# The last feed-forward's up projections of a two-block transformer kernel as seven block products, with the features between the projections split beside the second of them

## The reference

```python
x = x + jnp.concatenate([attn, pooled], axis=-1) @ w_out[l]
x = x + 0.5 * swiglu(rms_norm(x, ffn2_norm[l]), ffn2_w_gate[l], ffn2_w_up[l], ffn2_w_down[l])
# swiglu(x, g, u, d) = (silu(x @ g) * (x @ u)) @ d;  1024 -> 2816 twice, 2816 -> 1024
```

## Time and profile before

| | us |
|---|---|
| median of 3 runs (lowest, highest) | 2365.52 (2364.51, 2366.09) |
| span of the profiled execution | 2362.9 |
| TensorE busy in it | 2328.1 |
| VectorE, ScalarE, GpSimd busy | 1200.3, 878.0, 468.8 |
| TensorE's granted clock, mean share of full | 0.999 |

### The profile page before, as it was taken

One profiled execution on the slowest core, in us unless ns is written; L12 is line 12 of the kernel. 1 busy time (PEld: TensorE's weight loads), 2 busy tenths in 40 slices (PEclk: granted clock), 3 DMA queues, 4 the chain that ended last, 5 costly groups with the idle time before them and its releaser, 6 DMA issues.

```text
span 2362.9 us, 27596 instructions
## 1 busy us (share of the span) xinstructions
PE 2328.1 (99%) x11083; PEld 1893.2 (80%) x11083; DVE 1200.3 (51%) x1817; ACT 878.0 (37%) x1362; POOL 468.8 (20%) x475
## 2 busy tenths in 40 slices
PE   7999999999999999999999999999999999999999
PEld 5888877888787877777888888888887868888887
DVE  6555765555324456635545336444335984444423
ACT  4322345554223447733323234233225353323321
POOL 0111523445002048800000010000011870000000
PEclk9999999999999999999999999999999999999999
DMA  8664035656223210023233232333332212333322
GB/s 295 189 200 146 1 114 163 191 183 187 92 96 105 90 57 2 1 63 98 89 98 98 98 97 91 98 98 96 100 101 88 81 36 81 95 94 97 98 98 80
DMA packets 169333, 247.41 MB, mean 105 GB/s; under 512 B 14889, under 2 KB 110694, under 8 KB 169206
## 3 DMA queue, kind: packets, MB, share of 16 engines
q1 hardware_dynamic: 156276, 200.93, 26.5%
q0 software_dynamic: 12624, 44.54, 6.1%
q10 hardware_dynamic: 306, 0.19, 0.0%
HBM read 243.51 MB, written 2.10 MB: 104 GB/s over the span
## 4 chain that ended last, share of the span: by engine, by line
PE 87%; DVE 6%; POOL 3%; issue 2%; ACT 1%; DMA 1%; ACTq 0%; SPq 0%; POOLq 0%; DVEq 0%
PE ps L586 79%; DVE dsa_mask L2547 1%; POOL hg_k L2798 1%; PE ps L1050 1%; DVE w_lo L1957 1%; POOL nsa_p L2888 1%; PE ps L1066 1%; DVE small L2545 1%; DVE h_lo L2054 1%; PE ps L558 1%; PE ps L1040 0%; PE ps L1039 0%; PE ps L1281 0%; POOL nsa_b L2857 0%; PE ps L966 0%
## 5 line engine op out<-in xcount | busy, mean ns | idle before, releaser
L1957 DVE TENSOR_TENSOR w_lo<-w_raw,w_hi 128x1024 fp32r<-128x1024 f32 (+2 forms) x358 | 445.8, 1245 | 1004.7 <-ACT w_hi L1373 1004.4
L1373 ACT ACTIVATE w_hi<-w_raw 128x1024 fp32r<-128x1024 f32 (+2 forms) x364 | 380.7, 1046 | 1088.7 <-PE ps L586 1088.4
L586 PE MATMUL ps<-h_hi,w_hi 128*128 128x512 f32 (+1 forms) x1928 | 756.9, 393 | 4.9 <-DVE w_lo L1957 3.3
L586 PE MATMUL ps<-h_lo,w_hi 128*128 128x512 f32 (+1 forms) x1928 | 750.6, 389 | 0.0
L586 PE MATMUL ps<-h_hi,w_lo 128*128 128x512 f32 (+1 forms) x1928 | 750.4, 389 | 0.0
L586 PEld LDWEIGHTS ps<-h_hi,w_hi 128*128 128x128 f32 (+1 forms) x1928 | 361.3, 187 | 93.7 <-issue 7.6
L586 PEld LDWEIGHTS ps<-h_hi,w_lo 128*128 128x128 f32 (+1 forms) x1928 | 361.4, 187 | 76.4
L586 PEld LDWEIGHTS ps<-h_lo,w_hi 128*128 128x128 f32 (+1 forms) x1928 | 361.5, 187 | 75.9 <-issue 1.7
L586 PE MATMUL ps<-hid_hi,w_hi 128*128 128x512 f32 x616 | 240.9, 391 | 0.0
L586 PE MATMUL ps<-hid_lo,w_hi 128*128 128x512 f32 x616 | 239.7, 389 | 0.0
L586 PE MATMUL ps<-hid_hi,w_lo 128*128 128x512 f32 x616 | 239.7, 389 | 0.0
(11 more groups left out here) (397 smaller groups left out, 2570.0 us busy)
## 6 DMA issues: line engine op xcount, KB each, us to landing
w_raw<-in_ffn_w_up SPq DMA_DIRECT2D x264, 256.0 KB, 3.0
w_raw<-in_ffn_w_down SPq DMA_DIRECT2D x176, 256.0 KB, 2.8
m_raw<-in_ada_w POOLq DMA_DIRECT2D x80, 512.0 KB, 4.4
w_raw<-in_ffn_w_gate SPq DMA_DIRECT2D x88, 256.0 KB, 2.8
w_raw<-in_hg_w_in SPq DMA_DIRECT2D x64, 256.0 KB, 3.1
w_raw<-in_nsa_w_in SPq DMA_DIRECT2D x40, 256.0 KB, 2.9
w_raw<-in_w_in SPq DMA_DIRECT2D x32, 256.0 KB, 2.8
m_acc<-in_ada_w SPq DMA_DIRECT2D x9, 512.0 KB, 6.7
```

The source lines that it names most:

```text
L586: ins = K.nc.tensor.matmul(out, lhsT, rhs, start=start, stop=stop)
L1373: K.nc.scalar.activation(K.half(K.w_hi[u % SPL], width), K.half(K.w_raw[u % RAW], width), ACT.Copy) \
L1957: K.nc.vector.tensor_tensor(K.half(K.w_lo[u % SPL], width), K.half(K.w_raw[u % RAW], width), hi, ALU.subtract) \
```

## The change

It concerns `ffn_d` alone; elsewhere only names change. Gate and up weights by the two halves of the 1024 input features are a 2 x 2 matrix of blocks a11 (gate, first half), a12 (gate, second half), a21, a22 (up); the features by the early and the late 256 tokens are b11, b12, b21, b22. Instead of eight block products, a group makes seven (Strassen's scheme in Winograd's form), each 24 matmuls with 256 columns: the feature sums t1 to t4 are made once, the weight sums s1 to s4 for every group on GpSimd, from raw weights in float32, and the products' sums partly in PSUM, partly on VectorE.

- **Products** (`PRODUCTS`, `fast_order`): p1 = a11 b11, p5 = s1 t1, p6 = s2 t2, p7 = s3 t3, p4 = a22 t4, p3 = s4 b22, p2 = a12 b21. In groups 2 to 10 in the order p1, p6, p7, p5, p4, p3, p2; the first two groups begin with p1, p5 of group 0 and p1, p5 of group 1, which need the first half of the features alone. p4 is added in the bank of p7, p3 in that of p5, p2 in that of p1, each after that bank's first value has been read.
- **ScalarE**: split of product n + 3 into one of three pairs of buffers, then the copy of p1 out of PSUM (`u2`), and a group's Silu in one operation of 1024 elements.
- **VectorE**: the low part of product n + 3 ahead of what follows product n: the additions out of PSUM (u2, u3, up1, up0, gate1), the factors on the gate (gate0, gate2), the gating of 1024 elements.
- **GpSimd**: `third` (s3), `first` (s1), `second` (s2), `fourth` (s4) and `scaled` (the factors on the up half), 1024 elements each; before the first group also t1, t3 and t4 in two parts each.
- **SP**: four loads of 512 KB for a group into eight raw buffers, instead of eight of 256 KB into four.
- **The features between the projections** are kept in float32 (`hid`) and are split for each unit of the down projection, into a ring of two, by 1024 elements on ScalarE and on VectorE (`scalar_hid_high`, `vector_hid_low`), twice over, once for each half of the output. The first pair's low part is queued on VectorE after gate2 of group 10 and ahead of its gating.

The core of the diff; left out are the names of semaphores, the bookkeeping of loads and slots (`raw`, `hi`, `lo`, `raw_free`), and `hid_items`, which lists the down projection's matmuls as before over the ring.

```diff
+        self.hid = sb("hid", [P, KF, S], at=ar)
+        place = {"b11": ar + 45056, "t1": ar + 53248, "t2": ar + 61440, "t3": self.h_at, "t4": self.h_at + 8192,
+                 "b22": self.h_at + 16384, "b21": self.h_at + 24576}
+        self.feat = {n: sb(f"feat_{n}", [P, 4, 2, 256], F32R, at=at) for n, at in place.items()}
+        self.ring_hi = [sb(f"ring_hi{j}", [P, 2, S], F32R, at=self.h_at + 8192 * j) for j in range(2)]
+        self.ring_lo = [sb(f"ring_lo{j}", [P, 2, S], F32R, at=self.h_at + 8192 * j + 4096) for j in range(2)]
+        self.w_raw += [sb(f"w_raw{RAW + j}", [P, 1024], at=ar + 69632 + 4096 * j) for j in range(RAW)]
+        self.gate_buf = sb("gate_buf", [P, 2, S], at=ar + 86016)
+        self.u2 = [sb(f"u2_{j}", [P, 2, 256], at=ar + 90112 + 2048 * j) for j in range(2)]
+        self.s3, self.s2 = [sb(f"s3_{j}", [P, 1024], at=m + 16384 + 4096 * j) for j in range(2)], sb("s2", [P, 1024], at=m + 24576)
+        self.w_hi.append(sb("w_hi2", [P, 1024], F32R, at=m + 4096))
+        self.w_lo.append(sb("w_lo2", [P, 1024], F32R, at=m + 10240))
...
+        self.raw_1, self.raw_2 = sb("raw_1", [P, 4, S], at=ar), sb("raw_2", [P, 4, S], at=ar + 16384)
+        self.sums = {n: sb(f"sum_{n}", [P, 4, 256], at=ar + (8192 if n == "t1" else 28672 + 4096 * j)) for j, n in enumerate(("t1", "t2", "t3", "t4"))}
...
+                for g in range(UP_GROUPS):
+                    cols = slice(256 * g, 256 * g + 256)
+                    for n, (name, w, k) in enumerate((("a11", gate_w, 0), ("a21", up_w, 0), ("a22", up_w, 1), ("a12", gate_w, 1))):
+                        load((tag, g, name), [(slice(0, 4), slice(0, 256), w[rows[k], cols].rearrange("(kk p) c -> p kk c", p=P))],
+                             n + (0 if g % 2 else RAW))
+                self.unit[tag] = len(self.units)
+                for g, product in fast_order(tag):
+                    self.unit[tag, g, product] = unit(512, (tag, g, product), FAST_SPL)
...
+FAST = ("ffn_d",)
+FAST_SPL = 3
+PRODUCTS = {"p1": ("a11", "b11", "X"), "p2": ("a12", "b21", "X"), "p3": ("s4", "b22", "Y"), "p4": ("a22", "t4", "Z"),
+            "p5": ("s1", "t1", "Y"), "p6": ("s2", "t2", "W"), "p7": ("s3", "t3", "Z")}
+OPENING = ("p1", "p6", "p7", "p5")
+def fast_order(tag):
+    later = [(g, p) for g in range(2, UP_GROUPS) for p in ("p1", "p6", "p7", "p5", "p4", "p3", "p2")]
+    return [(g, p) for g in range(2) for p in ("p1", "p5")] + [(g, p) for g in range(2) for p in ("p6", "p7", "p4", "p3", "p2")] + later
+def first_rows(tag):
+    return (1, 0)
+def fast_bank(g, role):
+    if g < 2:
+        return ({"X": 4, "Y": 5, "W": 2, "Z": 3}, {"X": 6, "Y": 7, "W": 0, "Z": 1})[g][role]
+    return ({"X": 4, "W": 5, "Z": 7, "Y": 6}, {"X": 0, "W": 1, "Z": 2, "Y": 3})[g % 2][role]
...
+def tensor_fast_up(K, tag):
+    pe, ps, before = K.pe, K.ps, PLAIN_BEFORE[tag]
+    opened = {}
+    for n, (g, product) in enumerate(fast_order(tag)):
+        u, (_, feature, role) = K.unit[tag, g, product], PRODUCTS[product]
+        bank, opens = fast_bank(g, role), product in OPENING
+        if n == 0:
+            pe.wait_ge(*K["x_new"].at((before, norm_order(before)[3])))
+        elif (g, product) == (0, "p6"):
+            pe.wait_ge(*K["x_new"].at((before, norm_order(before)[7])))
+        elif (g, product) == (1, "p6"):
+            pe.wait_ge(*K["rstd"].at((before, "ln")))
+        if opens:
+            if bank in opened:
+                pe.wait_ge(*K["up_part"].at(opened[bank]))
+            opened[bank] = (tag, g, FREED_BY[role])
+        elif product == "p2":
+            pe.wait_ge(*K["first_copied"].at((tag, g)))
+        else:
+            pe.wait_ge(*K["up_part"].at((tag, g, "up1" if product == "p3" else "u3")))
+        pe.wait_ge(*K["w_low"].at(u))
+        hi, lo, moving = K.hi(u), K.lo(u), K.feat[feature]
+        for kt in range(4):
+            pe.wait_ge(*K["feature_low"].at((tag, feature, kt // 2)))
+            for f in range(2):
+                out, w = ps[:, bank, f * 256:f * 256 + 256], slice(kt * 256 + f * P, kt * 256 + (f + 1) * P)
+                K.nc.tensor.matmul(out, hi[:, w], moving[:, kt, 0, :], start=opens and kt == f == 0, stop=False, skip_group_check=True)
+                K.nc.tensor.matmul(out, hi[:, w], moving[:, kt, 1, :], start=False, stop=False, skip_group_check=True)
+                ins = K.nc.tensor.matmul(out, lo[:, w], moving[:, kt, 0, :], start=False, stop=kt == 3, skip_group_check=True)
+        ins.then_inc(*K["unit_multiplied"].up(u))
+        if n == 5:
+            tensor_plain_sum(K, before)
...
+def scalar_first_features(K, tag):
+    for n in range(4):
+        scalar_feature_raw(K, tag, n)
+    for name in ("b11", "t1"):
+        for j in range(2):
+            scalar_feature_high(K, tag, name, j)
+def scalar_second_features(K, tag):
+    u0 = K.unit[PLAIN[tag]]
+    for j in range(2):
+        scalar_feature_raw(K, tag, 4 + 2 * j)
+        if j:
+            scalar_split(K, u0 + 1)
+        scalar_feature_raw(K, tag, 5 + 2 * j)
+        scalar_feature_high(K, tag, "t2", j)
+    scalar_split(K, u0 + 2)
+    for m, name in enumerate(("t3", "t4", "b22", "b21")):
+        for j in range(2):
+            scalar_feature_high(K, tag, name, j)
+        if m == 0:
+            scalar_plain_square(K, tag, 4)
+            scalar_plain_square(K, tag, 5)
+            scalar_split(K, u0 + 3)
+        elif m == 1:
+            scalar_plain_square(K, tag, 6)
+            scalar_plain_square(K, tag, 7)
...
+    for n, (g, product) in enumerate(order):
+        if n:
+            scalar_split(K, first + n + 3)
+        if n == 4:
+            scalar_plain_rstd(K, PLAIN_BEFORE[tag])
+        act.wait_ge(*K["unit_multiplied"].at(first + n))
+        if product == "p1":
+            if g >= 2:
+                act.wait_ge(*K["up_part"].at((tag, g - 2, "gate1")))
+            nc.scalar.activation(K.u2[g % 2][:, :, :], K.ps[:, fast_bank(g, "X"), :].rearrange("p (f t) -> p f t", f=2), ACT.Copy) \
+                .then_inc(*K["first_copied"].up((tag, g)))
+        if ended is not None:
+            gate(ended)
+        ended = g if product == "p2" else None
+        if g == UP_GROUPS - 1 and product in ("p5", "p4"):
+            scalar_hid_high(K, tag, int(product == "p4"))
+    gate(ended)
...
+def vector_second_features(K, tag, gain):
+    order, u0 = norm_order(tag), K.unit[PLAIN[tag]]
+    for j in range(2):
+        two = slice(2 * j, 2 * j + 2)
+        for n in (4 + 2 * j, 5 + 2 * j):
+            vector_add_to_x(K, tag, order[n], gain)
+        if j:
+            vector_split(K, u0 + 1)
+        K.dve.wait_ge(*K["feature_raw"].at((tag, 5 + 2 * j)))
+        K.dve.wait_ge(*K["feature_made"].at((tag, "t1", j)))
+        K.nc.vector.tensor_tensor(K.sums["t2"][:, two, :], K.raw_2[:, two, 256:512], K.sums["t1"][:, two, :], ALU.subtract) \
+            .then_inc(*K["second_made"].up((tag, j)))
+    for j in range(2):
+        vector_feature_low(K, tag, "t2", j)
+    vector_split(K, u0 + 2)
+    for m, name in enumerate(("t3", "t4", "b22", "b21")):
+        for j in range(2):
+            vector_feature_low(K, tag, name, j)
+        if m == 0:
+            vector_plain_square_sum(K, tag, 4)
+            vector_plain_square_sum(K, tag, 5)
+            vector_split(K, u0 + 3)
+        elif m == 1:
+            vector_plain_square_sum(K, tag, 6)
+            vector_plain_square_sum(K, tag, 7)
...
+    def opened_by_fifth(g):
+        dve.wait_ge(*part(g, "u3"))
+        nc.vector.tensor_tensor(up(g)[:, :, late], up(g)[:, :, late], bank(g, "Y"), ALU.add).then_inc(*K["up_part"].up((tag, g, "up1")))
+    def bank(g, role):
+        return K.ps[:, fast_bank(g, role), :].rearrange("p (f t) -> p f t", f=2)
+    def gated(g):
+        dve.wait_ge(*K["silu"].at((tag, g)))
+        dve.wait_ge(*K["up_scaled"].at((tag, g)))
+        nc.vector.tensor_tensor(up(g), up(g), gate_buf[:, :, :], ALU.mult).then_inc(*K["hid_gated"].up((tag, g)))
+    order, ended = fast_order(tag), None
+    for n, (g, product) in enumerate(order):
+        if n:
+            vector_split(K, first + n + 3)
+        if ended is not None and product != "p1":
+            gated(ended)
+            ended = None
+        dve.wait_ge(*K["unit_multiplied"].at(first + n))
+        u2 = K.u2[g % 2][:, :, :]
+        if product == "p6":
+            dve.wait_ge(*K["first_copied"].at((tag, g)))
+            nc.vector.tensor_tensor(u2, u2, bank(g, "W"), ALU.add).then_inc(*K["up_part"].up((tag, g, "u2")))
+        elif product == "p7":
+            dve.wait_ge(*part(g, "u2"))
+            nc.vector.tensor_tensor(up(g)[:, :, late], u2, bank(g, "Z"), ALU.add).then_inc(*K["up_part"].up((tag, g, "u3")))
+            if g < 2:
+                opened_by_fifth(g)
+        elif product == "p5" and g >= 2:
+            opened_by_fifth(g)
+        elif product == "p4":
+            nc.vector.tensor_tensor(up(g)[:, :, early], u2, bank(g, "Z"), ALU.add).then_inc(*K["up_part"].up((tag, g, "up0")))
```

(68 more changed lines are left out.)

268 lines of the change are left out of this document (218 added, 50 removed).

## The result

| | before | after |
|---|---|---|
| median (lowest to highest), us | 2365.02 (2363.83 to 2366.09), 4 runs | 2427.14 (2426.34 to 2427.76), 4 runs |
| ratio of times, 95% interval | | 1.0262 (1.0247 to 1.0276) |
| span of the profiled execution | 2362.9 | 2425.3 |
| output projection's end | 1996.3 | 1999.0 |
| from there to the first unit of the down projection | 240.3 | 298.3 |

What follows compares the result with a forecast made beforehand. TensorE, busy 99% of the span, was taken as the bound. Start +31, steady groups +18 and end +5 gave +54 us on the 2365.5 median: 2420 us; own range 2405 to 2436, range given 2368 to 2437.

Steps and rivals of the forecast that it cites:

- The matmuls.: Up projections on TensorE: 256-column matmuls at 0.12 us, 20.16 us a group, saving 1.60 a group, 17.6 us in all.
- The rival by which a matmul of 256 columns costs 0.13: Up projections: the upper-bound matmul cost takes the whole saving; +9 us, 2429 or more; chance 4%.
- They don't fit together.: Up projections: VectorE and GpSimd operations with two SBUF operands exclude each other; 20.5 us per group at best.
- rival (a): Up projections: the port costs little, only latencies count, 23.1 against 17.6 us saved; +5.5, 2371 us; chance 15%.
- A steady group: Later up groups: p5, p4, p3 late by 1.5, 1.7, 0.5 us; period 24.0 us, eight groups +18 us.
- So it is full.: Shared SBUF port in each up group: 20.5 us of turns at best against TensorE's 20.16 us.
- The start.: First two up groups, from the output projection's end: 74.9 us against 43.5 before, +31 us, trusted 22 to 38.
- The end.: Up to down projection: hid's first split waits on VectorE behind the last product's work; +5.2 us.
- The down projection.: Added splits of 2.1 and 2.5 us per 5.44 us unit are hidden; priced at nothing with the stage's 127.6 us.
- The sum.: Whole kernel: +31, +18 and +5 make +54 us, added to the median of 2365.5 for 2420 us.
- Rival (b): Up projections: three split slots absorb the port's turns; 13.9 us saved, 5.2 lost at the end, 2357 us; chance 13%.

Runs made afterwards that it cites:

- e8_four: Changed kernel with VectorE's additions first, both edges of the up projections requeued, and all four weight sums on VectorE from group 3 on; 2370.4 us.
- e1_tiny: Changed kernel with GpSimd's four weight sums per group cut to 8 of 1024 columns, output incomplete; 2383.1 us.
- e2_memset: Changed kernel with each GpSimd weight sum replaced by a fill of the same tile that reads nothing from SBUF; 2384.5 us.
- e3_adds: Changed kernel with VectorE taking what follows a product out of PSUM before making the low part of product n + 3; 2402.9 us.
- e6_fill: Changed kernel with 60 idle matmuls put into TensorE's waits in the start, results never read; 2421.9 us.
- e4_early: Changed kernel with group 0's s3, s1, s2 made before the square sums, and the first two hid low parts made inside group 10; 2417.2 us.

## Why the prediction was right

By its own steps:

- **The matmuls.** 0.12 us, read from a matmul on 64 of the 128 rows, was right to the rounding: six groups of e8_four in 120.96 us give 0.1200. The rival by which a matmul of 256 columns costs 0.13 is refuted, and so is, for these matmuls, the estimate of 18.3 us a group from the figure in the Trainium skill, "TensorE: Matmul & The Clock Gate", section "Back-to-back issue gap". Seven products are worth 1.6 us a group, as said.
- **"They don't fit together."** Right, shown by e1_tiny and e2_memset: without the sums' turns the period is 20.67 us, which is rival (a)'s 20.16 and a wait of 0.41 for u3 (priced 0.43), plus 0.1 for the first matmul after a wait. Rival (a) was right about a group and the end, wrong in its premise. Its 14.0 us of latencies in the start were not seen by themselves: in e1_tiny the start is 24 us above its products, but the feature sums' turns and 7 us of slow products are in it.
- **A steady group.** Late by 1.5, 1.7 and 0.5 us as forecast, 1.60, 1.63 and 0.57 as measured; period 24.0 against 24.24, eight groups 192 against 194.3. The turns stand where the forecast put them: s3 ends 6.3 us into the group (forecast 6.0), gate2 6.8 (6.6). The last group is 20.8, not 21.5.
- **"So it is full."** This reason, that the port's 20.5 us a group stand against TensorE's 20.16, was not the one that counted. At the same load e3_adds had a period of 23.0. What cost was the second half of the same sentence: TensorE waits for VectorE in a chain, where a w_lo came late by a turn and, for 1.2 us of the period, stood ahead of the additions.
- **The start.** In us from the output projection's end, forecast and measured: p1 of group 0 6.8 and 6.6, p5 13.2 and 12.9, p1 of group 1 19.7 and 19.1, its p5 23.3 and 24.4, p6 of group 0 29.4 and 29.0, p4 41.2 and 40.1, p6 of group 1 49.8 and 51.1, p4 66.3 and 66.7, first product of group 2 74.9 and 78.0. The largest step that was mis-sized is the clock, "0 to +5 us, taken as 0": 4.0 us by e6_fill, whose start is 74.0. The forecast's 74.9 is right only for a clock that stays up. What it was compared with was 0.9 us too low: the old form's first two groups take 44.4 us, not 43.5, as the norm's two matmuls stand among them.
- **The end.** 5.2 and 5.2; e4_early takes it away.
- **The down projection.** Priced at nothing beside 127.6, which was read at a cut 1.2 us too early: 126.3 before, 128.0 after. 1.3 us of the difference are the clock, at whose lower level the first matmuls ran after the wait of 5.2 us: in e4_early, without that wait, the stage takes 126.7.
- **The sum.** 54 us forecast for the up part and its end, 58.0 measured: 4.0 more for the clock, 0.9 less for the rest of the start, 0.9 less for the old form's 44.4, 2.3 more for the eight groups, 0.7 less for the last, and rounding. With 2.7 us upstream, 1.7 in the down projection and 0.8 less outside the span (1.8 us for 2.6) that is the 7 us by which 2427.1 lies above 2420. That the total came within 0.3% is in part luck: the terms that nobody foresaw, 2.7 us upstream among them, are small, and some cancel. The forecast's own range, "2405 to 2436", is 2406 to 2437 by its terms.
- **Rival (b)**, that the turns are absorbed, did not come about: at p5 and at p4 the blocked operations were on the chain.

## What to carry to other kernels

Before giving an idle GpSimd the elementwise work of a busy VectorE, count the operations on both sides that read two operands from SBUF: here each sum on GpSimd cost VectorE at least as much time as making it, and moving all four back took the steady period from 23.0 to 20.16 us. On the engine that others wait for, queue what frees the tensor engine ahead of what prepares work three steps on: that order alone was worth 24 us. And weigh a scheme that saves arithmetic by its fixed costs: with half the columns a matmul seven products for eight gave 7% of a stage, 12 us here with the waits for u3 and 18 without any. The first two groups, with the extra sums, gave 11 us or more of it back in every version, and no version was measurably faster than the kernel before.

## What the runs showed of the hardware

- A matmul with its own weight load takes 0.2267 us with 512 columns and 0.1200 with 256, at full clock: some 13 ns beyond the columns' time at 2.4 GHz. At the lower level 256 columns take 0.213 to 0.215 us, which leaves next to none.
- GpSimd's fills of 1804 ns and VectorE's w_lo run side by side: w_lo takes 1.21 to 1.23 us under them.
- The block is by instruction, not by size: in e1_tiny GpSimd's in-place sum of 8 columns took 1207 ns on average, in the same kernel the other 8-column sums 203 to 204, since it was issued just after a w_lo had begun (at 2146.20 after 2146.13) and ended with it.
- A turn hurts both. In e8_four `scaled`, alone on GpSimd, takes 3910 ns instead of 2400, and VectorE loses 1.8 us a group to it (12 sums at 1768 ns and 19 w_lo at 1431 where 1217 is undisturbed, over six groups), which is hidden there.
- In the changed kernel the slow products follow waits of TensorE of 2.1 to 9.9 us; after the steady groups' waits of 0.6 to 1.6 us none is slow. In e3_adds two of the five products behind a wait of 2.2 us ran slow. The low clock's price is less than the slow products' extra time (4.0 of 9.6 us): when e6_fill took 8.8 us off the products, the waits between them grew by 4.8.
